# Mixer entry of a fused transformer kernel: order of the last down units, of the first token half's transposes and of a weight subtraction; forget-gate columns in two rounds

## The reference, cut to what matters

```python
def shared_kv(h, kv_norm, w_kv, w_f, b_f):
    hn = rms_norm(h, kv_norm)
    k, v = jnp.split(hn @ w_kv, 2, axis=-1)
    log_f = jax.nn.log_sigmoid((hn @ w_f + b_f).astype(jnp.float32))   # w_f: 1024 x 16

# second block
h = modulate(rmsnorm(x, norm_ffn1[l]), sh1, sc1)
x = x + 0.5 * g1[:, None, :] * swiglu(h, ffn1_w_gate[l], ffn1_w_up[l], ffn1_w_down[l])
h = modulate(rmsnorm(x, norm_mix[l]), sh2, sc2)
x = x + g2[:, None, :] * hybrid_mixer(h, positions, w_in[l], ...)
```

## Time and profile before

| | PE | DVE | ACT | POOL |
|---|---|---|---|---|
| busy us | 1148.2 | 853.6 | 652.4 | 89.5 |
| share of the span | 98% | 73% | 56% | 8% |

### The profile page before, as it was taken

The page is one execution under the profiler, slowest core; times in us unless marked ns, Lnnn a source line. Parts: engine busy times, 40 slices in busy tenths (PEclk is TensorE's granted clock), DMA queues, the critical chain, the costliest instruction groups (busy, mean ns, idle before and its releaser), DMA issues.

```text
span 1167.0 us, 17601 instructions
## 1 busy us (share of the span) xinstructions
PE 1148.2 (98%) x6735; PEld 996.3 (85%) x6735; DVE 853.6 (73%) x1231; ACT 652.4 (56%) x900; POOL 89.5 (8%) x133
## 2 busy tenths in 40 slices
PE   8999999999999999999999999999999999999997
PEld 8887888888879788888888888888998889888895
DVE  7676799888767678988486665567986877655555
ACT  5654655565556555555575444556757765544453
POOL 9200011110000001110000000005000000000000
PEclk9999999999999999999999999999999999999999
DMA  8744699997453369997645555644651153665550
GB/s 270 233 137 157 210 341 362 322 320 251 139 189 124 96 216 354 345 332 247 212 133 192 193 204 193 202 134 149 199 185 69 46 188 129 217 209 187 175 203 36
DMA packets 143207, 236.32 MB, mean 203 GB/s; under 512 B 6341, under 2 KB 106918, under 8 KB 143142
## 3 DMA queue, kind: packets, MB, share of 16 engines
q1 hardware_dynamic: 130258, 196.47, 50.5%
q0 software_dynamic: 10368, 37.75, 8.8%
q10 hardware_dynamic: 2516, 1.22, 0.4%
HBM read 234.37 MB, written 1.05 MB: 202 GB/s over the span
## 4 chain that ended last, share of the span: by engine, by line
PE 87%; DVE 6%; ACT 3%; issue 2%; DMA 1%; POOL 0%; POOLq 0%; ACTq 0%; DVEq 0%
PE ps L2645 18%; PE ps L2364 9%; PE ps L2648 9%; PE ps L2366 9%; PE ps L2368 9%; PE ps L2309 4%; PE ps L2203 3%; PE ps L2211 3%; PE ps L2204 3%; DVE wlo L1281 2%; PE ps L2282 2%; PE ps L2283 2%; PE ps L2284 2%; PE ps L2470 1%; PE ps L2472 1%
## 5 line engine op out<-in xcount | busy, mean ns | idle before, releaser
L1281 DVE TENSOR_TENSOR wlo<-raw,whi 128x2048 fp32r<-128x2048 f32 (+2 forms) x180 | 405.2, 2263 | 120.3 <-ACT whi L677 120.0
L677 ACT ACTIVATE whi<-raw 128x2048 fp32r<-128x2048 f32 (+2 forms) x180 | 338.2, 1889 | 128.9 <-PE ps L2648 42.9
L2645 PE MATMUL ps<-a,whi 128*128 128x512 f32 x1024 | 255.8, 392 | 0.0
L2645 PEld LDWEIGHTS ps<-a,whi 128*128 128x128 f32 x1024 | 186.6, 188 | 35.6 <-issue 0.2
L2648 PEld LDWEIGHTS ps<-a,wlo 128*128 128x128 f32 x1024 | 139.7, 190 | 10.0
L2648 PE MATMUL ps<-a,wlo 128*128 128x256 f32 x1024 | 142.8, 282 | 0.0
L2364 PE MATMUL ps<-whi,hh 128*128 128x512 f32 x352 | 109.3, 392 | 0.5 <-DVE wlo L1281 0.5
L2366 PE MATMUL ps<-wlo,hh 128*128 128x512 f32 x352 | 108.7, 390 | 0.0
L2368 PE MATMUL ps<-whi,hl 128*128 128x512 f32 x352 | 108.6, 390 | 0.0
L1827 DVE SCALAR_TENSOR_TENSOR stage<-stage,cact 128x1024 f32<-128x1024 f32 x63 | 80.7, 1281 | 3.5 <-DMA stage<-in_w_ada_dram 2.0
L2366 PEld LDWEIGHTS ps<-wlo,hh 128*128 128x128 f32 x352 | 66.1, 188 | 14.2
(11 more groups left out here) (474 smaller groups left out, 1987.3 us busy)
## 6 DMA issues: line engine op xcount, KB each, us to landing
stage<-in_w_ada_dram POOLq DMA_DIRECT2D x72, 512.0 KB, 5.8
raw<-in_w_up_dram SPq DMA_DIRECT2D x32, 1024.0 KB, 7.3
raw<-in_w_down_dram SPq DMA_DIRECT2D x32, 1024.0 KB, 7.8
raw<-in_ffn_w_gate_dram SPq DMA_DIRECT2D x22, 1024.0 KB, 5.3
raw<-in_ffn_w_up_dram SPq DMA_DIRECT2D x22, 1024.0 KB, 5.3
raw<-in_ffn_w_down_dram SPq DMA_DIRECT2D x22, 1024.0 KB, 5.1
raw<-in_moba_w_qkv_dram SPq DMA_DIRECT2D x11, 1024.0 KB, 7.2
raw<-in_w_in_dram SPq DMA_DIRECT2D x10, 1024.0 KB, 5.2
```

The lines of the kernel that those rows point to most:

```text
L677: A.activation(whi[:, s, 0:size], raw[:, s, 0:size], ACT.Copy).then_inc(w_hi, 1)
L1281: V.tensor_tensor(wlo[:, s, 0:size], raw[:, s, 0:size], whi[:, s, 0:size].bitcast(F32), ALU.subtract).then_inc(w_lo, 1)
L2645: T.matmul(bank(b + m), wh[:, c, m * P:(m + 1) * P], a2[:, c].rearrange("p k n -> p (k n)"), start=(c == 0), stop=False)
```

## The change

- The first swiglu's `last_units` is called with `between_halves`: low columns of the three down units, then the high columns, and behind the first unit's high columns PE does the eight transposes of the first half (`mix_T(0, ...)`), each block once. The twelve repeated transposes go.
- DVE scales the lower 512 columns of the first half's `xn`, ACT the upper 512, as both did for the second half; `xn_dve` is counted up three times for each entry instead of twice.
- `mix_parts` takes the place of `gated_parts`: the subtraction of unit `U_TAIL + 1` stands behind the low-column residual of the second half, then come the splits of two pairs for tokens 0 to 127, then the high-column residual, the norm and the scaling.
- ACT's `half_gained` does two pairs, one behind the other.
- `tail_half` takes two units (the spare one and `U_TAIL + 1`), for t = 0 and for t = 1, in the order high weights first, then the low ones behind a wait for the unit's subtraction. `d_unit` is left with two units.
- The gate columns are done in two rounds: in the first the two matmuls of each block that need only the high part, behind `in_hi`; in the second the eight with the low part, behind `in_ready`.

```diff
             def part_norm(b, ahead=None):
...
                     if ahead and t == 1:
                         splits(U_TAIL + 1)
                         part_square(b, t, 0)
-                        half_gained(*ahead)
+                        for j in range(2):
+                            half_gained(j, *ahead)
                         part_square(b, t, 1).then_inc(sq_part, 1)
...
-                    cols = slice(512 * t, D)
+                    cols = slice(512, D)
...
-            def gated_parts(idx, b):
-
-                for t in range(TT):
-                    gated_part(idx, b, t)
-                    if t == 1 and b == PART["mix"]:
-                        dve.wait_ge(half_hi, 1)
-                        half_split(0).then_inc(half_in, 1)
-                    part_rstd(b, t)
+            def mix_parts(idx, b):
+
+                gated_part(idx, b, 0)
+                part_rstd(b, 0)
+                part_scale(b, 0)
+                gated_part(idx, b, 1, (0,))
+                splits(U_TAIL + 1)
+                for j in range(2):
+                    dve.wait_ge(half_hi, j + 1)
+                    half_split(j, 0).then_inc(half_in, 1)
+                gated_part(idx, b, 1, (1,))
+                part_rstd(b, 1)
                 part_scale(b)
...
             dve.wait_ge(gate_done, 1)
-            gated_parts(4, PART["mix"])
-            splits(U_TAIL + 1)
+            mix_parts(4, PART["mix"])
             gained("mix", ah, al, *mod(1))
...
                             last_units([(u + 1 + q, hh[:, q], hl[:, q], 0) for q in range(3)],
-                                       [(h_ready, c0 + CH2 - 2 + q) for q in range(3)])
+                                       [(h_ready, c0 + CH2 - 2 + q) for q in range(3)], at_end)
...
+            o = ps[0:H, 3, 0:S]
+            for c in range(CT):
+                if c % 2 == 0:
+                    pe.wait_ge(in_hi, PAIR0["kv"] + c // 2 + 1)
+                T.matmul(o, wfh[:, c], ah[:, c], start=(c == 0), stop=False)
+                T.matmul(o, wfl[:, c], ah[:, c], start=False, stop=False)
             for c in range(CT):
                 if c % 2 == 0:
                     pe.wait_ge(in_ready, PAIR0["kv"] + c // 2 + 1)
-                o = ps[0:H, 3, 0:S]
-                T.matmul(o, wfh[:, c], ah[:, c], start=(c == 0), stop=False)
-                T.matmul(o, wfh[:, c], al[:, c], start=False, stop=False)
-                ins = T.matmul(o, wfl[:, c], ah[:, c], start=False, stop=(c == CT - 1))
+                ins = T.matmul(o, wfh[:, c], al[:, c], start=False, stop=(c == CT - 1))
...
-            def tail_half(t):
+            def tail_half(u, t):
...
+                for lo in range(2):
+                    if lo:
+                        unit_wait(U_TAIL + u)
+                    for k in range(2):
+                        for x_, w_ in ((ah, wl),) if lo else ((ah, wh), (al, wh)):
...
-            mix = PART["mix"]
-            pe.wait_ge(xn_act, 2)
-            mix_T(0, range(2)).then_inc(half_tr, 1)
-            for _ in range(2):
-                mix_T(0, range(2, CT))
-            unit_wait(U_TAIL)
-            pe.wait_ge(half_in, 1)
-            tail_half(0)
-            mix_T(1, range(CT), {0: (xn_dve, mix + 1), 4: (xn_act, 3)})
-            pe.wait_ge(in_ready, PAIR0["mix"] + 1)
-            tail_half(1).then_inc(w_used, 1)
-            for u in range(1, 4):
+            swiglu(U_FFN1, CHUNK0["ffn1"], "ffn1", 1, lambda: mix_T(0, {0: (xn_dve, 2), 4: (xn_act, 2)}))
+            for u in range(2):
+                pe.wait_ge(half_in, u + 1)
+                pe.wait_ge(w_hi, U_TAIL + u + 1)
+                tail_half(u, 0)
+            mix_T(1, {0: (xn_dve, 3), 4: (xn_act, 3)})
+            for u in range(2):
+                pe.wait_ge(in_ready, PAIR0["mix"] + u + 1)
+                tail_half(u, 1).then_inc(w_used, 1)
+            for u in range(2, 4):
                 d_unit(U_TAIL + u, slot(U_TAIL + u), 0, 2, TAILW, ah, al, 2 * u, False, u == 3, "mix")
```

More of the change, by code:

```diff
@@ L733, in gained @@
                         c = 2 * j + q
-                        n0 = P if stage_name == "mix" and j == 0 else 0
+                        n0 = P if stage_name == "mix" and j < 2 else 0
                         src = ps[:, bank_of[j], q * S + n0:(q + 1) * S]
@@ L773, in root_table, with half_gained @@
                 A.activation(newt[:, 4, 3:4], ident[:, 0:1], ACT.Sqrt)
[L775 to L779, removed]
+            def half_gained(j, gain, shift):
+                act.wait_ge(half_tr, j + 1)
+                for q in range(2):
+                    c = 2 * j + q
+                    ins = A.activation(tmp2[:, j, q * S:q * S + P], ps[:, TBANK[j], q * S:q * S + P], ACT.Identity,
                                        scale=gain(c), bias=shift(c))
@@ L1356, in gained @@
                     dve.wait_ge(in_hi, PAIR0[stage_name] + j + 1)
-                    if stage_name == "mix" and j == 0:
-                        ins = half_split(1)
+                    if stage_name == "mix" and j < 2:
+                        ins = half_split(j, 1)
                     elif shift is None:
@@ L1409, in entry, with half_split @@
                     token_group(e, 1, i)
-            def half_split(t):
+            def half_split(j, t):
                 tt = slice(t * P, t * P + P)
-                v = tmp2[:, 0].rearrange("p (c n) -> p c n", c=2)[:, :, tt]
-                link(V.tensor_copy(ah[:, 0:2, tt], v))
-                return V.tensor_tensor(al[:, 0:2, tt], v, ah[:, 0:2, tt].bitcast(F32), ALU.subtract)
+                v = tmp2[:, j].rearrange("p (c n) -> p c n", c=2)[:, :, tt]
+                link(V.tensor_copy(ah[:, 2 * j:2 * j + 2, tt], v))
+                return V.tensor_tensor(al[:, 2 * j:2 * j + 2, tt], v, ah[:, 2 * j:2 * j + 2, tt].bitcast(F32), ALU.subtract)
             def plain(stage_name, j, hi, lo):
@@ L2409, in token_T @@
                     elif c == 0:
-                        pe.wait_ge(xn_dve, 2 * e + 1)
+                        pe.wait_ge(xn_dve, 3 * e + 1)
                     elif c == 4 and t == 1:
@@ L2697, in mlp, with swiglu @@
                 last_d_unit(n0 + N_MLP - 1, slot(n0 + N_MLP - 1), hh[:, 0], hl[:, 0], 0)
-            def swiglu(n0, c0, stage_name, gates):
+            def swiglu(n0, c0, stage_name, gates, at_end=None):
                 def pair(u, i, k):
@@ L2803, in _, with mix_T @@
             mlp(U_MLP1, CHUNK0["mlp1"], "mlp1", ADA0, ADA1)
-            swiglu(U_FFN1, CHUNK0["ffn1"], "ffn1", 1)
-            def tail_half(t):
+            def tail_half(u, t):
                 tt = slice(t * P, (t + 1) * P)
-                wh, wl = (w[:, 0:2 * TAILW].rearrange("p (c n) -> p c n", c=2) for w in (bhf, blf))
+                if u == 0:
+                    wh, wl = (w[:, 0:2 * TAILW].rearrange("p (c n) -> p c n", c=2) for w in (bhf, blf))
+                else:
+                    wh, wl = (w_view(w, slot(U_TAIL + u), 2, TAILW) for w in (whi, wlo))
                 outs = [(ps[:, 2 * t + v // 512, 0:min(512, TAILW - v)], v, min(v + 512, TAILW))
                         for v in range(0, TAILW, 512)]
[L2811 to L2815, removed]
-                return ins
-            def mix_T(t, cs, ready=None):
-                for c in cs:
+                for lo in range(2):
[3 more added lines that the diff above has]
+                        for x_, w_ in ((ah, wl),) if lo else ((ah, wh), (al, wh)):
+                            for o, v, e in outs:
+                                ins = T.matmul(o, x_[:, 2 * u + k, tt], w_[:, k, v:e],
+                                               start=(u == 0 and k == 0 and not lo and x_ is ah), stop=False)
+                return ins
+            def mix_T(t, ready=None):
+                for c in range(CT):
                     if ready and c in ready:
@@ L2823, in mix_T @@
                     ins = T.transpose(o, xn[:, t, c * P:(c + 1) * P], ident[:])
-                    if t == 1 and c % 2 == 1:
-                        ins.then_inc(tr_done, 1)
-                return ins
-            mix = PART["mix"]
-            pe.wait_ge(xn_act, 2)
-            mix_T(0, range(2)).then_inc(half_tr, 1)
-            for _ in range(2):
-                mix_T(0, range(2, CT))
-            unit_wait(U_TAIL)
-            pe.wait_ge(half_in, 1)
-            tail_half(0)
-            mix_T(1, range(CT), {0: (xn_dve, mix + 1), 4: (xn_act, 3)})
-            pe.wait_ge(in_ready, PAIR0["mix"] + 1)
-            tail_half(1).then_inc(w_used, 1)
-            for u in range(1, 4):
+                    if c % 2 == 1:
+                        if t == 1:
+                            ins.then_inc(tr_done, 1)
+                        elif c < 4:
+                            ins.then_inc(half_tr, 1)
+            swiglu(U_FFN1, CHUNK0["ffn1"], "ffn1", 1, lambda: mix_T(0, {0: (xn_dve, 2), 4: (xn_act, 2)}))
[8 more added lines that the diff above has]
+            for u in range(2, 4):
```

4 lines of the change are left out of this document (2 added, 2 removed).

## The result

| | kernel before | changed kernel |
|---|---|---|
| median | 1169.14 us (1168.37 to 1170.15, 22 runs) | 1170.99 us (1170.28 to 1172.52, 22 runs) |
| profiled execution | 1168.64 | 1171.64 |
| its span | 1167.0 | 1170.0 |

The ratio is 1.0017, with a 95% interval from 1.0011 to 1.0023: slower by 1.85 us. Forecast were 1171.9, or +2.66. The direction and the places are right, and the size is 0.8 us too large; at 0.16% the difference lies just inside the 0.2% that the chances used as their border, where the text had given 0.24.

The account below looks back on a forecast made before the run. PE, busy 1148.2 of 1167.0 us, was taken as the bound. Entry stage +3.0 less 0.36 at the gate columns gave +2.66; on 1168.64 that is 1171.3, plus 0.56 to the median 1171.9 us, range 1169.7 to 1173.4.

Parts of the forecast that it names:

- part 1: Last down units: new column order and eight transposes release the middle unit 2.2 us later, at 788.53; 0.66 of transposes saved.
- part 2: Mixer entry: copy, subtraction, then splits in a row; PE's first wait grows from 1.51 to 3.2 us.
- price of 1.58: Moved subtraction without POOL's slowdown, by the rule that only SBUF-reading GpSimd operations block DVE; sum would be 0.2 us less.
- part 3: Second token half: transposes start at 798.05 after a 0.75 us wait, product at 800.4, 3.8 us later than before.
- part 4: Rest of first projection: PE waits from 804.7 to 805.9 for the third unit's subtraction; stage ends 3.0 us later.
- the sum: Stage 3.0 us longer less 0.36 at the gate columns: +2.66, giving 1171.9 us.
- part 5: Gate columns in two rounds: gain 0.36 us, at least 0, at most 1.1.
- Covered: Rival at the entry: DVE's work is covered, all waits and six transposes go, 3.8 us less, 1165.4; chance 0.06.
- No difference: Rival: release at 788.5 holds but operations behind it are shorter than their rows; +1.5, 1170.7; chance 0.24.
- The clock: Rival: clock falls in the longer entry wait, slowing first-half products; +3.5 on top, 1175.4; chance 0.10.

Follow-up runs that it names:

- e7: The kernel before with POOL's tile work held back until the fourth tail unit is used: 1168.80 us.
- e8: The changed kernel with 24 more transposes in PE's long wait, so PE is never idle there for more than a few tenths: 1170.98 us, ratio 1.0018.
- e4: e3 with DVE's high-column residual of the second half also ahead of the subtraction: 1168.36 us, ratio 0.9993.
- e3: e2 with ACT's square of the low columns and both gains also ahead of the copy of the second tail unit: 1169.61 us, ratio 1.0007.
- e6: The changed kernel with POOL's tile work held back until the fourth tail unit is used: 1172.23 us.
- e2: The changed kernel with both first-half splits ahead of the second tail unit's subtraction on DVE, ACT's list untouched: 1172.51 us, ratio 1.0029.
- e12: The changed kernel with POOL's tile work held back until the eighth tail unit is used: 1170.74 us, ratio 1.0013.

## Why the prediction was right, and where its size was off

**Release of the middle down unit (part 1): right.** Forecast 2.2 later; ACT's copy came within 0.01 of the forecast instant, closer than rows read from another execution can be relied on. Undoing this part alone gave back 0.84.

**Subtraction ahead of the split (part 2): the mechanism right, the size not.** DVE idled for 3.66 and released PE. The forecast had PE start at 793.59 in after's frame; it started at 793.09, and the first wait was 2.53, not 3.2 (0.5 of that is the earlier start, and the rest is that the wait is counted from the modelled end of the last matmul, 790.56, and not from 790.39). This is a term that was mis-sized, in two operations: the subtraction took 1.59, not 1.78, and the first split 0.77 from start to start (792.19 to 792.96), not 1.05. Both values had been kept at what they cost beside POOL's additions. The price of 1.58 that the prediction worked out from the page, and did not use, was right to 0.01, but its reason was not: POOL's selects read SBUF too, as they read and write `place`. What happened beside the subtraction stands in POOL's rows, the changed kernel's first and below it the kernel before with POOL held to the fourth unit (e7), where the same two selects met no such subtraction:

```profile
790.98 1.79 POOL L650 TENSOR_SCALAR_AFFINE_SELECT place<-place 128x64 f32<-128x64 f32 x2
```

```profile
811.50 0.63 POOL L650 TENSOR_SCALAR_AFFINE_SELECT place<-place 128x64 f32<-128x64 f32 x2
```

The subtraction had started 0.3 earlier, at 790.68, and kept its length; the selects took 1.2 longer. One pair later it was the other way round: a select of POOL (0.41) started at 793.39, the second split's subtraction at 793.43, and this took 0.66 instead of 0.43. The Trainium skill, "SBUF — State Buffer", section "SBUF: two separate sides", says that of a DVE operation with two SBUF inputs and a GpSimd operation that reads SBUF the one that starts first has the shared port pair for its whole length, and the other waits. Both places of the trace agree.

**Residual, norm, transposes, second split (part 3): right within 0.3.** With the clock at 1.00 throughout (e8, shifted so that the first residual operations fall together) the transposes come at 798.23 in after's frame, forecast 798.54, and the second half's product at 800.60, forecast 800.89. In the changed kernel's own profile they come at 798.72 and 800.96, since the slow clock held PE's products until then.

**Third unit (part 4): the wait came, at half its size.** Forecast 1.2, measured 0.52. The step that failed is the sentence that POOL stays beside this stretch in either kernel. POOL is quicker after the change, where DVE stands idle for longer beside it, and is done at 801.16:

```profile
794.53 4.96 POOL L659 TENSOR_TENSOR hh<-place,selr 128x128 fp32r<-128x128 f32 x12
799.46 1.70 POOL L659 TENSOR_TENSOR hl<-place,selr 128x128 fp32r<-128x128 f32 x4
```

Twelve additions take 4.96 where they took 7.54, and DVE's pairs 2 and 3 run without them, at 1.07 to 1.09 each instead of 1.35 and the subtraction at 1.59 instead of 1.75: 0.7 less. Of this 0.2 went to something that the sum had left out: DVE waited 0.28 for ACT's gains ahead of pair 2.

**The sum.** With the clock held the stage is 2.24 longer (33.61 against 31.37), not 3.0. Less the gate columns' 0.35 that is 1.89, and 1.85 was measured; as the one comes from two single profiles and the other from medians, an agreement to 0.04 is partly luck. Durations taken beside POOL's additions were 1.2 too long in all: 0.2 for the subtraction, 0.3 for the first split (the second took the forecast 1.05), 0.6 for pairs 2 and 3 and 0.2 for the last subtraction. Against them stand 0.4 that the sum had too short: residual, norm, and the wait for ACT's gains. That leaves the 0.8.

**The gate columns (part 5): right**, 0.35 of 0.36 in the stage.

**The rivals.** "Covered" did not come, and the order of e4 shows what it wanted: ACT's gains ahead of the copy. "No difference" was written down as this very case, the release holding and the operations behind it shorter because POOL's slowdown goes, with +1.5; the measured +1.85 lies between it and the forecast. The chance of 0.24 was too low beside a price that I had called uncertain from both sides. The clock did fall in the profiled execution, but its price of 3.5 was far too high: 0.3 in that stage, because it lasted 3.4 us and ran beside DVE's row, and 0.8 in the medians of the executions with a lower mean clock.

What stays open: why e3 is 0.3 above its range; what the column order and the early transposes are worth in the faster kernels; and why POOL doubles the small steps of the latent norm (128x4, 0.16 to 0.32), while of the five steps of the mixer's norm (128x1) beside the same additions in the changed kernel four keep their 0.15 to 0.27 and only the last grows, from 0.16 to 0.28. In e6 the steps of the latent norm start 0.36 apart, which is also the pace of POOL's additions beside them (4.33 for twelve).

## What to carry to other kernels

An operation moved forward in one engine's list brings nothing while what it reads is made by another engine behind a wait: follow the buffer's release through every queue (here PE's third unit, ACT's copy, DVE's subtraction) and move the independent work of all of them ahead of the waiting instruction. When one engine frees its columns in another order, look for who waits for a whole unit of it. And take a duration from a row in which the neighbour engine does what it will do after the change, since a moved gap also moves the neighbour's work.

## What the runs showed of the hardware

- DVE and POOL slow each other both ways. The same split took 0.29 and 0.43 alone and up to 0.57 and 0.66 beside POOL; twelve of POOL's additions took 7.54 beside a busy DVE, 4.96 beside a half idle one and 4.33 beside DVE's small steps. Where a DVE subtraction and a select of POOL met, the one that had started first kept its length: the subtraction of 1376 columns stayed at 1.59 while two selects took 1.79 instead of 0.63, and a subtraction of 256 columns that started 0.04 after a select took 0.66 instead of 0.43.
- PE's granted clock went from 1.00 to 0.50 near 792.8, after an idle time that began at 790.6, and was back at 796.2, with PE busy again from 793.1. In e2 it fell at 801.0, after idle times of 2.41 and 2.67. Idle times of 1.5 and 1.3 had not done this in the kernel before, nor one of 2.41 in the profiles of e6 and e12.
- Repeating 24 transposes in a wait keeps the clock and costs nothing on the path, but is worth only what lies uncovered behind the wait: here 0.3 of the stage, and nothing in the median.
